# A two-layer hybrid block with a routed expert layer: gate products spread over 78 expert tiles, 30 gathers ahead, picks over 192 pairs

## The chip, the core and the metric

The kernel runs on one core of a Trainium2 chip. The metric is the device time of one execution in microseconds (us). The core has a matrix engine (TensorE, PE; its weight loads are shown as PEld), VectorE (DVE), ScalarE (ACT), GpSimd (POOL), SyncE (SP), which here only issues transfers, and 16 DMA engines. SBUF has 128 partitions; PSUM, into which the matrix engine writes, has 8 banks of 512 fp32 words in each partition.

## What is computed

Two layers over 512 tokens of width 1024. Each layer is a token mixer (a projection, a chunked scan, pooling, stick-breaking attention, an output projection) and then a routed expert layer, which the change is about. Cut to that:

```python
def peer_ffn(h, w_q, keys, u_tab, v_tab):
    q = (ht @ w_q).reshape(t, 8, 2, 128)
    sc = jnp.einsum('thid,hikd->thik', q, keys)           # 128 keys for each half
    top_s, top_i = lax.top_k(sc, 16)
    cand = top_s[:, :, 0, :, None] + top_s[:, :, 1, None, :]
    best_s, best_pos = lax.top_k(cand.reshape(t, 8, 256), 16)
    i1 = jnp.take_along_axis(top_i[:, :, 0], best_pos // 16, axis=-1)
    i2 = jnp.take_along_axis(top_i[:, :, 1], best_pos % 16, axis=-1)
    experts = i1 * 128 + i2                               # of 16384 experts
    gates = jax.nn.softmax(best_s, axis=-1)
    act = jnp.einsum('thkd,td->thk', u_tab[experts], h)
    return jnp.einsum('thk,thkd->td', gates * gelu(act), v_tab[experts])
```

## The kernel before

**Two ways to the experts.** For the first 160 tokens the rows of the chosen experts are fetched. Such a gather is an indirect DMA that brings one row of 1024 words (4 KB) for each partition, 512 KB in all. There are 160 of them from the u table and 160 from the v table in each layer (`UG`); DVE multiplies a u row by the token and sums it (`gather_u`), and adds a v row into a sum (`gather_v`). For the other 352 tokens (`TD`) all 16384 experts are computed. The u table comes as 128 tiles of 512 KB. In a **u tile** PE runs 24 matmuls of 352 columns: 8 steps of the inner dimension, each as high part by high part, high part by low part and low part by high part of the fp32 numbers. Behind the 128 u tiles come 128 v tiles of the same size.

**A u tile on each engine.** SP loads the tile into one of three raw slots (`load_w`). ACT copies it rounded to the high part (`hi`, line 765). DVE or, for tiles 2 to 38 of a layer, POOL subtracts to get the low part (`lo`, lines 1620 and 706). Both have two slots, so the parts of tile n+2 can be made only after tile n is done. PE multiplies (line 1047), and ACT takes the result through a gelu into `act_out` (line 977), from where SP stores two tiles at a time to DRAM.

**Routing.** In tiles 0 to 41 DVE turns the scores into experts and gates, in four groups of 128 tokens (`tt`). The step `picked` finds the index that belongs to each of the 128 chosen pairs of a token: a comparison (line 2212), a product (2214) and a sum (2218) over 128 x 16 elements, twice a group. Between them DVE consumes the first u gathers (`EARLY_GATHERS`: 14), of which POOL issues 16 in the tiles of `POOL_GATHER_AT`, each behind its low part. DVE then waits for POOL's last low part (tile 38) and takes over the low parts in its loop from tile 37 on, which in each turn n also consumes `U_GATHERS[n]` gathers.

**Gates.** A token's gates are needed as a matrix over all experts, 128 x 128 for each token. It is the product of two one-hot matrices, one of which carries the gates. Four tokens are a **quad**; there are 88. For a quad, DVE builds the one-hots (`one_hots`, line 2142, 1024 wide, one of `OH_SLOTS` = 4 slots), ACT scales one half by the gates (line 970, four instructions), PE runs four fp32 products of 128 x 128 (lines 1547 and 1561; the trace shows two instructions for each) behind the u tile, and ACT copies them from PSUM to `stages` (line 1001). `quads_of(n)` says which quads lie behind tile n: one or two by turns from tile 42 (`GATE0`) to 101. The gates of 224 of the 352 tokens go to DRAM in four chunks of 14 quads, each in four stores in four tiles one after another (`stores_of`), and come back in groups for the v tiles (`load_gates`, `load_acts`).

**Gather slots.** The gathered rows lie in a ring of five slots. POOL issues a gather once DVE has used the one five before (`s_gd`).

**PE's loops.** Tiles 42 to 97 are seven turns of a loop with eight tiles in it, then four tiles are written out, then a loop of two tiles runs to 127.

In every queue the instructions run in the order of the code: a wait on DVE for a gather holds all that DVE has behind it.

## Time and profile before

| | |
|---|---|
| median of three runs | 2907.31 us (2906.72 to 2907.58) |
| the profiled execution | 2909.28 us |
| its span, first to last instruction | 2907.5 us |
| busy: PE, PEld, DVE, ACT, POOL | 99%, 92%, 86%, 50%, 34% |
| granted PE clock, mean share of full | 0.997 |
| moved by DMA | 854.89 MB, mean 294 GB/s |

The stages, by the trace's time: layer 1 has its mixer to about 290 us, the key scores to 398, u tiles from 398 to 977 (the gate stretch from 569), v tiles to 1475. Layer 2 has the same at 1475 to 1719, 1809, 1809 to 2392 (gates from 1981) and 2890. In a row of a view, the engine, the line of the kernel, the operation and the tiles that it writes and reads come first; behind `<-` stands what ended a wait.

### The profile page before, as it was taken

The numbers are of one execution on the slowest core, as the hardware profiler recorded it, in microseconds if no ns is written. First come the engines' busy times: TensorE is split into PE (matmuls) and PEld (weight loads), VectorE is DVE, ScalarE is ACT, GpSimd is POOL, SyncE is SP. The second block draws the span as 40 slices with busy tenths as digits, with TensorE's granted clock in tenths as the row PEclk, the third lists the DMA queues.
The fourth block names the chain that finished last, engine by engine and source line by source line (L and its number), as shares of the span: only waits on it lengthen the run. The fifth ranks groups of instructions, "written<-read, shape, count | busy, mean of one in ns | idle before, by whom it ended". The sixth has DMA issues, their size and how long they took to land.

```text
span 2907.5 us, 49129 instructions
## 1 busy us (share of the span) xinstructions
PE 2864.6 (99%) x17864; PEld 2679.3 (92%) x17864; DVE 2495.4 (86%) x4770; ACT 1445.8 (50%) x2309; POOL 995.8 (34%) x773
## 2 busy tenths in 40 slices
PE   7999999999999999999999999999999999999998
PEld 4777789999999999999988788999999999999998
DVE  4667789799996899999986779989999879999998
ACT  3345234488883433334353532447888634333333
POOL 1000027644443343444400000675444433443442
PEclk9999999999999999999999999999999999999999
DMA  7435647899999999999932122679999999999996
GB/s 278 169 114 185 256 150 240 302 366 381 389 333 381 351 382 379 380 387 383 378 118 66 66 73 80 208 241 354 393 369 367 347 378 355 387 378 382 378 383 252
DMA packets 252524, 854.89 MB, mean 294 GB/s; under 512 B 25568, under 2 KB 58592, under 8 KB 245728
## 3 DMA queue, kind: packets, MB, share of 16 engines
q1 hardware_dynamic: 149280, 442.23, 41.7%
q0 software_dynamic: 98496, 381.73, 35.2%
q10 hardware_dynamic: 4608, 29.36, 2.4%
q8 instruction: 52, 0.85, 0.1%
q14 instruction: 88, 0.72, 0.1%
HBM read 777.06 MB, written 76.15 MB: 293 GB/s over the span
## 4 chain that ended last, share of the span: by engine, by line
PE 84%; DVE 7%; DMA 5%; ACT 2%; issue 1%; POOL 0%; SPq 0%; DVEq 0%; ACTq 0%; POOLq 0%
PE banks L1047 40%; PE banks L1579 30%; PE banks L1547 4%; DMA ring<-u,gidx 3%; DMA w_raw<-wst 2%; PE banks L1380 2%; DVE w_lo L1620 2%; PE banks L1117 2%; DVE ring L2120 1%; PE banks L1467 1%; PE banks L1063 1%; ACT w_hi L765 1%; DVE oneh L2142 1%; DMA ada_buf<-adaw 1%; DVE vacc L2132 0%
## 5 line engine op out<-in xcount | busy, mean ns | idle before, releaser
L765 ACT ACTIVATE w_hi<-w_raw 128x1024 fp32r<-128x1024 f32 x596 | 630.3, 1058 | 751.4 <-PE banks L1047 651.6
L1047 PE MATMUL banks<-hH,w_hi 128*128 128x352 f32 (+1 forms) x2528 | 867.4, 343 | 3.2 <-DVE w_lo L1620 1.9
L1620 DVE TENSOR_TENSOR w_lo<-w_raw,w_hi 128x1024 fp32r<-128x1024 f32 x522 | 639.0, 1224 | 263.6 <-ACT w_hi L765 259.9
L1047 PE MATMUL banks<-hH,w_lo 128*128 128x352 f32 (+1 forms) x2528 | 846.2, 335 | 0.0
L1047 PE MATMUL banks<-hL,w_hi 128*128 128x352 f32 (+1 forms) x2528 | 846.2, 335 | 0.0
L718 POOL DMA_INDIRECT ring<-v,gidx x320 | 396.8, 1240 | 593.3 <-DVE vacc L2132 532.3
L718 POOL DMA_INDIRECT ring<-u,gidx x320 | 395.4, 1235 | 466.3 <-DVE gact L2120 450.2
L1047 PEld LDWEIGHTS banks<-hH,w_hi 128*128 128x128 f32 x2528 | 475.5, 188 | 50.6 <-issue 20.6
L1579 PE MATMUL banks<-c_lo_late,w_hi 128*128 128x352 f32 x1536 | 494.2, 322 | 0.0
L1047 PEld LDWEIGHTS banks<-hH,w_lo 128*128 128x128 f32 x2528 | 474.8, 188 | 19.5
L1047 PEld LDWEIGHTS banks<-hL,w_hi 128*128 128x128 f32 x2528 | 475.8, 188 | 17.4 <-issue 0.5
L2132 DVE SCALAR_TENSOR_TENSOR vacc<-ring,gcoef,vacc 128x1024 f32<-128x1024 f32 x316 | 404.7, 1281 | 7.1
L2120 DVE CUSTOM_DVE_ANT_0 ring<-ring,banks 128x1024 f32<-128x1024 f32 x256 | 304.9, 1219 | 52.2 <-DMA ring<-u,gidx 27.8
L706 POOL TENSOR_TENSOR w_lo<-w_raw,w_hi 128x1024 fp32r<-128x1024 f32 x74 | 177.8, 2402 | 468.4 <-ACT w_hi L765 468.4
L1579 PE MATMUL banks<-c_hi_late,w_hi 128*128 128x352 f32 x1024 | 334.8, 327 | 2.6 <-DVE w_lo L1620 2.2
L1579 PE MATMUL banks<-c_hi_first,w_hi 128*128 128x352 f32 x1024 | 332.6, 325 | 0.0
L1579 PE MATMUL banks<-c_hi_first,w_lo 128*128 128x352 f32 x1024 | 331.0, 323 | 0.0
L1579 PE MATMUL banks<-c_hi_late,w_lo 128*128 128x352 f32 x1024 | 330.1, 322 | 0.0
L1579 PEld LDWEIGHTS banks<-c_lo_late,w_hi 128*128 128x128 f32 x1536 | 289.3, 188 | 0.0
L970 ACT ACTIVATE oneh<-oneh,idxT 128x128 f32<-128x128 f32 x704 | 214.9, 393 | 6.8 <-DVE oneh L2142 5.1
L2142 DVE TENSOR_TENSOR oneh<-iota,idxT 128x1024 f32<-128x1024 f32 x176 | 210.3, 1223 | 0.0
L1022 ACT ACTIVATE c_hi_late<-coef 128x352 fp32r<-128x352 f32 x128 | 63.8, 499 | 289.0 <-DVE coef L2292 289.0
(347 smaller groups left out, 4013.1 us busy)
## 6 DMA issues: line engine op xcount, KB each, us to landing
w_raw<-wst SPq DMA_DIRECT2D x596, 512.0 KB, 6.5
activations<-act_out SPq DMA_DIRECT2D x124, 352.0 KB, 8.2
act_in<-activations SPq DMA_DIRECT2D x62, 704.0 KB, 7.9
gate_matrices<-stages ACTq DMA_DIRECT2D x32, 896.0 KB, 9.3
gates<-gate_matrices SPq DMA_DIRECT2D x64, 448.0 KB, 9.6
ada_buf<-adaw POOLq DMA_DIRECT2D x24, 1024.0 KB, 6.8
nrm<-adaw POOLq DMA_DIRECT2D x8, 1024.0 KB, 5.2
pj<-adaw POOLq DMA_DIRECT2D x7, 1024.0 KB, 7.2
```

The costliest lines, as they stand in the source:

```text
L706: pool.tensor_tensor(w_lo[g % 2][:, :, :].rearrange("p a b -> p (a b)"), w_raw[:, g % RAWS, :], w_hi[g % 2][:, :, :].rearrange("p a b -> p ...
L718: pool.indirect_dma_start(out=ring[:, n % RING, :], out_offset=None, in_=rows[:, :], in_offset=bass.IndirectOffsetOnAxis(ap=gidx[:, k % UG ...
L765: nc.scalar.activation(w_hi[g % 2][:, :, :].rearrange("p a b -> p (a b)"), w_raw[:, g % RAWS, :], ACT.Copy).then_inc(s_wh, 1)
L970: ins = nc.scalar.activation(oh, oh, ACT.Copy, scale=idxT[:, 2, q * QUAD + t:q * QUAD + t + 1])
L1022: nc.scalar.activation(c_hi[(b + 2) % GROUP], coef[:, b % 2, :], ACT.Copy).then_inc(s_chi, 1)
L1047: last = mm(bank[s][:, 0:t.stop - t.start], a[s][:, k, :], b[:, k, t], start=(k == 0 and a is w_hi and b is hH), stop=(k == KT - 1 and a i ...
L1547: last = mm(bank[2 + u % 2][:, t * P:(t + 1) * P], oneh[u % OH_SLOTS][:, 0, t, :], oneh[u % OH_SLOTS][:, 1, t, :], start=True, stop=True)
L1579: last = mm(bank[k][:, TG:T], w[j % 2][:, k, :], c[j], start=(first and w is w_hi and c is c_hi), stop=(final and w is w_lo))
L1620: v.tensor_tensor(w_lo[g % 2][:, :, :].rearrange("p a b -> p (a b)"), w_raw[:, g % RAWS, :], w_hi[g % 2][:, :, :].rearrange("p a b -> p (a ...
L2120: v.tensor_tensor_reduce(ring[:, n % RING, :], ring[:, n % RING, :], rhs, 1.0, 0.0, ALU.mult, ALU.add, gact[:, k:k + 1]).then_inc(s_gd, 1)
L2132: ins = v.scalar_tensor_tensor(acc[:, :], ring[:, n % RING, :], gcoef[:, k:k + 1], acc[:, :], ALU.mult, ALU.add)
L2142: v.tensor_tensor(oneh[q % OH_SLOTS][:, :, :, :], iota[:, :].unsqueeze(1).unsqueeze(1).broadcast_to(full), idxT[:, 0:2, q * QUAD:(q + 1) * ...
```

## The change

Quads lie behind tiles 42 to 119, one a tile, and two in ten of them (`DOUBLE`). PE's loop holds 16 tiles and runs four times, and 14 tiles are written out. The one-hots have three slots, at another place. The first 30 u gathers of a layer land in 12 slots inside `stages`, which is unused until the first copies, and no longer in the ring; POOL issues 26 of them in tiles 11 to 38, DVE uses 20 in the routing stretch and the other ten in tiles 37 to 41. In DVE's loop the one-hots come ahead of the gathers. SP's first loads for the v tiles move from tiles 110, 112 and 116 to 116, 124 and 126. `picked` leaves out, for the eight best pairs, the indices that they can't have: 8 x 8 + 8 x 16 = 192 in place of 256 for each head, in two instructions in place of one. The matrices of a quad are laid out in PSUM by token in layer 1 (as before) and by expert in layer 2, where PE so writes with a step of four words; the copy to `stages` writes four neighbouring words at a time in both.

```diff
--- before.py
+++ after.py
@@ -94,9 +94,11 @@
 GATE0 = 42
-GATE1 = 102
-GATE_LOOP = 8
-OH_SLOTS = 4
+GATE1 = N_KEYS - 8
+GATE_LOOP = 16
+GATE_LOOPS = 4
+DOUBLE = [*range(7, 72, 8), 75]
+OH_SLOTS = 3
 
@@ -108,8 +110,8 @@
     i = n - GATE0
-    first = i // 2 * 3 + i % 2
-    return [q for q in ([first] if i % 2 == 0 else [first, first + 1]) if q < QUADS]
+    first = i + len([d for d in DOUBLE if d < i])
+    return [first, first + 1] if i in DOUBLE else [first]
 
@@ -138,19 +140,22 @@
 GATHERS = 2 * UG
-EARLY_GATHERS = (0, 4, 5, 5)
+EARLY_GATHERS = (0, 6, 7, 7)
 EARLY = sum(EARLY_GATHERS)
-POOL_GATHER_AT = [12, 13, 14, 15, 16, 20, 21, 22, 23, 28, 29, 30, 31, 32, 36, 37]
+AHEAD = 30
+AHEAD_SLOTS = 12
+AHEAD_FROM = 4
+AHEAD_SET = 4
+POOL_GATHER_AT = [11, 12, 13, 14, 15, 16, 17, 18, 19, 20, 21, 22, 23, 24, 25, 26, 27, 28, 29, 30, 31, 33, 34, 35, 37, 38]
 U_GATHERS = [0] * N_KEYS
 for _n in range(GATHER0, GATE0):
-    U_GATHERS[_n] = 1 if _n % 2 else 2
-for _n in range(GATE0, GATE1):
-    U_GATHERS[_n] = 2 if len(quads_of(_n + 1)) < 2 or _n % 4 == 2 else 1
-for _n in range(GATE1, N_KEYS - 1):
-    U_GATHERS[_n] = 2 if _n % 5 in (1, 3) else 1
-U_GATHERS[GATE1 + 4] = U_GATHERS[GATE1 + 14] = 1
-assert sum(U_GATHERS) + EARLY == UG and U_GATHERS[N_KEYS - 1] == 0, sum(U_GATHERS)
-POOL_GATE_LO = []
+    U_GATHERS[_n] = 2
+assert EARLY + sum(U_GATHERS) == AHEAD and len(POOL_GATHER_AT) <= AHEAD and POOL_GATHER_AT[-1] < GATHER0 + 2
+for _n in range(GATE0, N_KEYS - 1):
+    U_GATHERS[_n] = 1 if len(quads_of(_n + 1)) > 1 or _n == N_KEYS - 2 or _n % 2 and _n % 3 and _n + 1 < GATE1 else 2
+for _n in range(N_KEYS - 4, GATE0, -9):
+    U_GATHERS[_n] -= sum(U_GATHERS) > UG - EARLY and U_GATHERS[_n] > 1
+assert sum(U_GATHERS) + EARLY == UG and U_GATHERS[N_KEYS - 1] == 0, (UG - EARLY, sum(U_GATHERS))
 V_GATHERS = [0] + [2 if _b % 4 == 3 or _b in (33, 65, 97) else 1 for _b in range(1, N_KEYS - 1)] + [0]
@@ -397,11 +402,24 @@
         r3 = ExitStack()
-        oneh = [sb(f"oneh{s}", [P, 2, QUAD, P], where=r3) for s in range(2)]
+        sb("r3_gates", [P, GSTORED * GROUP * GCHUNK], where=r3)
+        oneh = [sb("oneh0", [P, 2, QUAD, P], where=r3)]
+        sb("r3_low", [P, 2048 - 1024 - GSTORED * GROUP * GCHUNK], where=r3)
         stages = sb("stages", [P, 2, N_KEYS, GWIDE], where=r3)
-        sb("r3_idx", [P, 20256 - 18432], where=r3)
-        oneh += [sb(f"oneh{s}", [P, 2, QUAD, P], where=r3) for s in range(2, OH_SLOTS)]
+        sb("r3_route", [P, 19776 - 18432], where=r3)
+        oneh += [sb(f"oneh{s}", [P, 2, QUAD, P], where=r3) for s in range(1, OH_SLOTS)]
         r3.close()
+
+        def gather_slot(l, k):
+
+            if k < AHEAD:
+                i = AHEAD_FROM + k % AHEAD_SLOTS
+                return stages[:, i // 8, :, :].rearrange("p e t -> p (e t)")[:, i % 8 * D:(i % 8 + 1) * D]
+            return ring[:, (l * (GATHERS - AHEAD) + k - AHEAD) % RING, :]
+
+        def by_expert(l, q):
+
+            return bank[2 + q % 2][:, :].rearrange("p (t e) -> p e t" if l == 0 else "p (e t) -> p e t", t=QUAD)
 
...
@@ -549,6 +567,7 @@
         s_g = [sem(f"gathered{s}") for s in range(RING)]
+        s_ga_in = [sem(f"gathered_ahead{s}") for s in range(AHEAD_SLOTS // AHEAD_SET)]
         s_gd = sem("gathered_used")
@@ -574,6 +593,16 @@
 
+        def gather_sem(l, k):
+
+            if k < AHEAD:
+                i = k % AHEAD_SLOTS // AHEAD_SET
+                uses = [j for j in range(AHEAD) if j % AHEAD_SLOTS // AHEAD_SET == i]
+                landed = len([j for j in uses if j // AHEAD_SLOTS <= k // AHEAD_SLOTS])
+                return s_ga_in[i], 16 * (l * len(uses) + landed)
+            n = l * (GATHERS - AHEAD) + k - AHEAD
+            return s_g[n % RING], 16 * (n // RING + 1)
+
         block = ctx.enter_context(nc.Block())
@@ -634,15 +663,15 @@
                         sp.dma_start(keys[:, :, :], keysT[l]).then_inc(s_keys, 16)
-                    if n == U0 + GATE1 + 8:
-
+                    if n == EV0 - 12:
                         for s in range(2):
                             sp.wait_ge(s_gst[s], (l + 1) * (GSTORED // 2) * STORES * 16)
+                        load_gates(l, 0)
+                    if n == EV0 - 4:
+
                         sp.wait_ge(s_gv, (l + 1) * QUADS + 2)
                         load_acts(l, 1)
-                    if n == U0 + GATE1 + 10:
-                        load_gates(l, 0)
-                    if n == U0 + GATE1 + 14:
+                    if n == EV0 - 2:
                         load_gates(l, 1)
@@ -709,16 +738,17 @@
 
-                n = l * GATHERS + k
-                if n >= RING:
-                    pool.wait_ge(s_gd, n - RING + 1)
+                if AHEAD_SLOTS <= k < AHEAD:
+                    pool.wait_ge(s_gd, l * GATHERS + k - AHEAD_SLOTS + 1)
+                if k >= AHEAD + RING:
+                    pool.wait_ge(s_gd, l * GATHERS + k - RING + 1)
                 if k == HK:
                 pool.indirect_dma_start(
-                    out=ring[:, n % RING, :], out_offset=None, in_=rows[:, :],
+                    out=gather_slot(l, k), out_offset=None, in_=rows[:, :],
                     in_offset=bass.IndirectOffsetOnAxis(ap=gidx[:, k % UG:k % UG + 1], axis=0)
-                ).then_inc(s_g[n % RING], 16)
+                ).then_inc(gather_sem(l, k)[0], 16)
 
@@ -735,19 +765,8 @@
                         gather(l, POOL_GATHER_AT.index(n - U0))
-                k = len(POOL_GATHER_AT)
-                used = EARLY
-                for n in range(GATHER0, GATE1):
-                    used += U_GATHERS[n]
-                    if n + 2 in POOL_GATE_LO:
-                        pool.wait_ge(s_wl, l * STREAM + U0 + n + 2)
-                        lo(l, U0 + n + 2)
-                    while k < used + RING:
-                        gather(l, k)
-                        k += 1
-                while k < GATHERS:
+                for k in range(len(POOL_GATHER_AT), GATHERS):
                     gather(l, k)
-                    k += 1
 
...
@@ -999,8 +1019,7 @@
                         nc.scalar.activation(
-                            home[:, :, i * QUAD:(i + 1) * QUAD].rearrange("p e t -> p t e"),
-                            bank[2 + q % 2][:, :].rearrange("p (t e) -> p t e", t=QUAD),
+                            home[:, :, i * QUAD:(i + 1) * QUAD], by_expert(l, q),
                             ACT.Copy).then_inc(s_gv, 1)
@@ -1534,7 +1553,14 @@
                 steps.settle()
-                per = GATE_LOOP // 2 * 3
+                per = GATE_LOOP // 8 * 9
+                def gate_quad(u):
+
+                    oh = oneh[u % OH_SLOTS]
+                    for t in range(QUAD):
+                        last = mm(by_expert(l, u)[:, :, t], oh[:, 0, t, :], oh[:, 1, t, :], start=True, stop=True)
+                    last.then_inc(s_gm, 1)
+
                 def gate_tiles(i, tiles):
@@ -1543,12 +1569,9 @@
                             pe.wait_ge(s_gv, l * QUADS + u + 1 + i * per)
-                            for t in range(QUAD):
-                                last = mm(bank[2 + u % 2][:, t * P:(t + 1) * P], oneh[u % OH_SLOTS][:, 0, t, :],
-                                          oneh[u % OH_SLOTS][:, 1, t, :], start=True, stop=True)
-                            last.then_inc(s_gm, 1)
-
-                loops = (GATE1 - GATE0) // GATE_LOOP
+                            gate_quad(u)
+
+                loops = GATE_LOOPS
                 with pe.Fori(0, loops) as i:
@@ -1557,10 +1580,7 @@
                         pe.wait_ge(s_gv, l * QUADS + u + 1)
-                        for t in range(QUAD):
-                            last = mm(bank[2 + u % 2][:, t * P:(t + 1) * P], oneh[u % OH_SLOTS][:, 0, t, :],
-                                      oneh[u % OH_SLOTS][:, 1, t, :], start=True, stop=True)
-                        last.then_inc(s_gm, 1)
+                        gate_quad(u)
                 with pe.Fori(GATE1 // 2, N_KEYS // 2) as i:
@@ -2114,22 +2134,22 @@
 
-                    n = l * GATHERS + k
-                    dve.wait_ge(s_g[n % RING], (n // RING + 1) * 16)
+                    dve.wait_ge(*gather_sem(l, k))
                     rhs = banks[:, 6:8, :].rearrange("p a t -> p (a t)") if k < HK else htok2[:, :]
-                    v.tensor_tensor_reduce(ring[:, n % RING, :], ring[:, n % RING, :], rhs, 1.0, 0.0,
-                                           ALU.mult, ALU.add, gact[:, k:k + 1]).then_inc(s_gd, 1)
+                    row = gather_slot(l, k)
+                    v.tensor_tensor_reduce(row, row, rhs, 1.0, 0.0, ALU.mult, ALU.add, gact[:, k:k + 1]).then_inc(s_gd, 1)
 
                     n = l * GATHERS + UG + k
-                    dve.wait_ge(s_g[n % RING], (n // RING + 1) * 16)
+                    dve.wait_ge(*gather_sem(l, UG + k))
+                    row = gather_slot(l, UG + k)
                     acc = vacc if k < HK else vacc2
                     if k in (0, HK):
-                        ins = v.tensor_scalar(acc[:, :], ring[:, n % RING, :], gcoef[:, k:k + 1], None, ALU.mult)
+                        ins = v.tensor_scalar(acc[:, :], row, gcoef[:, k:k + 1], None, ALU.mult)
                     else:
                         dve.wait_ge(s_gd, n)
-                        ins = v.scalar_tensor_tensor(acc[:, :], ring[:, n % RING, :], gcoef[:, k:k + 1], acc[:, :],
+                        ins = v.scalar_tensor_tensor(acc[:, :], row, gcoef[:, k:k + 1], acc[:, :],
                                                      ALU.mult, ALU.add)
@@ -2209,13 +2229,23 @@
                                         (col_at, iota[:, 0:TOPK], ALU.is_equal, row_at))[a]
-                    link(v.tensor_tensor(pk, at.unsqueeze(2).broadcast_to([P, HK, TOPK]),
-                                         of.unsqueeze(1).broadcast_to([P, HK, TOPK]), op))
-                    link(v.tensor_tensor(pk4, pk4, rows.unsqueeze(2).broadcast_to(full), ALU.mult))
+                    boxes = [(slice(0, 8), 8), (slice(8, TOPK), TOPK)]
+                    by_rank = lambda t: t.rearrange("p (h k) -> p h k", h=PH)
+                    for ranks, w in boxes:
+                        box = [P, PH, 8, w]
+                        ins = v.tensor_tensor(pk4[:, :, ranks, 0:w], by_rank(at)[:, :, ranks].unsqueeze(3).broadcast_to(box),
+                                              of[:, 0:w].unsqueeze(1).unsqueeze(1).broadcast_to(box), op)
+                    link(ins)
+                    for ranks, w in boxes:
+                        ins = v.tensor_tensor(pk4[:, :, ranks, 0:w], pk4[:, :, ranks, 0:w],
+                                              rows[:, :, 0:w].unsqueeze(2).broadcast_to([P, PH, 8, w]), ALU.mult)
+                    link(ins)
                     if a == 0 and tt >= 2:
                         dve.wait_ge(s_rtt, l * (NT - 1) + tt - 1)
-                    link(v.reduce_sum(route[:, a, :], pk, AX.X))
+                    for ranks, w in boxes:
+                        ins = v.reduce_sum(by_rank(route[:, a, :])[:, :, ranks], pk4[:, :, ranks, 0:w], AX.X)
+                    link(ins)
 
@@ -2304,21 +2334,18 @@
                 for n in range(GATHER0, N_KEYS):
-                    for _ in range(U_GATHERS[n]):
-                        gather_u(k)
-                        k += 1
                     if n == GATE0 - 1:
                         one_hots(q)
+                    for _ in range(U_GATHERS[n]):
+                        gather_u(k)
+                        k += 1
                     if n == N_KEYS - 2:
                         coefs(n - (N_KEYS - 2))
-                    if n + 2 not in POOL_GATE_LO:
-                        if n + 1 in POOL_GATE_LO:
-                            dve.wait_ge(s_wl, l * STREAM + U0 + n + 2)
-                        lo(l, U0 + n + 2)
+                    lo(l, U0 + n + 2)
                     if n >= N_KEYS - 2:
```

## Rows read from the trace of the kernel before

**Rows 1.** Busy time by stage: window, its length, each engine's busy time, PE clock, DMA.

```profile
398.00:570.00 172.00, 171.59 (x1066) 166.03 (x1063) 151.00 (x500) 73.84 (x102) 114.61 (x62) 1.00 0.72 233
570.00:875.00 305.00, 304.16 (x2120) 303.34 (x2119) 288.67 (x357) 267.41 (x558) 135.68 (x106) 1.00 0.97 368
875.00:978.00 103.00, 103.00 (x652) 103.00 (x652) 74.50 (x102) 39.10 (x57) 41.09 (x35) 1.00 1.00 381
...
1985.00:2290.00 305.00, 303.07 (x2104) 302.51 (x2103) 285.52 (x354) 265.17 (x553) 136.43 (x104) 0.99 0.97 363
```

**Rows 2.** Chain that ended last, merged: start us, length us, what.

```profile
561.79 11.73 PE banks L1047 x72
...
585.06 3.80 PE banks L1047 x24
...
590.64 3.81 PE banks L1047 x24
...
595.34 3.81 PE banks L1047 x24
...
875.09 102.61 PE banks L1047 x648
...
1981.31 4.25 PE banks L1047 x24
...
2289.63 102.61 PE banks L1047 x648
```

**Rows 3.** The same chain, where layer 2 loses time.

```profile
1968.47 10.21 DMA ring<-u,gidx
...
2135.74 17.93 DMA ring<-u,gidx
...
2154.92 2.29 DVE oneh L2142 x2
...
2160.39 4.92 PE banks L1047 x24
```

**Rows 4.** Busy time in shorter windows, columns as in rows 1.

```profile
600.00:620.00 20.00, 20.00 (x142) 20.00 (x140) 20.00 (x27) 17.68 (x39) 9.83 (x8) 1.00 0.93 341
...
720.00:740.00 20.00, 20.00 (x141) 20.00 (x140) 15.99 (x20) 17.49 (x37) 7.64 (x6) 1.00 1.02 420
...
900.00:930.00 30.00, 30.00 (x191) 30.00 (x190) 22.00 (x31) 11.29 (x16) 13.37 (x11) 1.00 1.03 406
```

**Rows 5.** Transfers of the page: issuer, count, KB each, median us to landing.

```profile
activations<-act_out SPq DMA_DIRECT2D x124, 352.0 KB, 8.2
...
gate_matrices<-stages ACTq DMA_DIRECT2D x32, 896.0 KB, 9.3
```

**Rows 6.** Timeline of ACT and POOL in layer 2's routing: start us, length us.

```profile
1850.23 1.06 ACT L765 ACTIVATE w_hi<-w_raw 128x1024 fp32r<-128x1024 f32 x1 [2.71 <-PE banks L1047]
...
1851.43 2.40 POOL L706 TENSOR_TENSOR w_lo<-w_raw,w_hi 128x1024 fp32r<-128x1024 f32 x1 [1.73 <-ACT w_hi L765]
...
1857.85 0.95 POOL L718 DMA_INDIRECT ring<-u,gidx  x1
```

**Rows 7.** Groups by line, DVE, 570 to 875 us: count, busy us, mean ns, idle.

```profile
L2142 DVE TENSOR_TENSOR oneh<-iota,idxT 128x1024 f32<-128x1024 f32 x88 | 105.1, 1223 | 0.0
```

**Rows 8.** Waits of DVE, 410 to 570 us: us in total, times, longest.

```profile
DVE ring L2120 <- POOL w_lo L706: 11.5, 1, 11.5
```

**Rows 9.** Groups by line, DVE's picks, 398 to 570 us.

```profile
L2214 DVE TENSOR_TENSOR pick<-pick,banks 128x2048 f32<-128x2048 f32 x8 | 18.3, 2288 | 0.3
```

**Rows 10.** Groups by line, ACT, 570 to 875 us.

```profile
L1001 ACT ACTIVATE stages<-banks 128x512 f32<-128x512 f32 x87 | 94.8, 1167 | 0.0
...
L977 ACT ACTIVATE act_out<-banks 128x352 f32<-128x352 f32 x59 | 26.3, 446 | 0.6 <-DMA activations<-act_out 0.6
```

**Rows 11.** Instructions of the gather line, 875 to 978 us: issue to landing.

```profile
DMA to landing us min/median/max: 5.5/7.7/9.1
```

**Rows 12.** All waits of DVE, 875 to 980 us.

```profile
DVE w_lo L1620 <- ACT w_hi L765: 31.1, 27, 2.1
```

5 lines of the change are left out of this document (3 added, 2 removed).

## Prediction

> **What bounds the kernel now.** I read the busy time by stage first [rows 1]. In both layers, from the start of the expert-score stage (398 and 1809 us) to the end of the second expert stage, TensorE (PE) works in nearly every microsecond: 304.2 of 305.0 in the gate stretch of layer 1, 303.1 of 305.0 in layer 2, all of the 103.0 behind it in layer 1. So the time there is that of the PE instructions, and what can be gained is only what PE loses between them. A PE busy time is blind to short losses, so the chain of waits is read next, for the pitch of the tiles [rows 2]. A u tile with nothing behind it takes 3.80 us (102.61 for 27). With one quad of one-hot products it takes 4.70 (590.64 to 595.34), with two 5.58 (585.06 to 590.64). One quad is thus 0.89 us wherever it lies. Sixty tiles from tile 42 on, of which 30 carry one quad, 29 two and one none, should take 30 x 4.70 + 29 x 5.58 = 302.8 up to the last of them. In layer 1 the chain has tile 40 at 561.79 and tile 101 at 875.09: 313.3, less two bare tiles (7.6) leaves 305.7, so **2.9 us are lost**. In layer 2 tile 42 stands at 1981.31 and tile 101 at 2289.63: 308.3, **5.5 us lost**. Some 0.3 of each is a change of datatype or rounding. The 26 tiles behind lose nothing.
>
> Where the loss comes from shows in the chain [rows 3]. A gather issued at 2135.7 takes 17.9 us to land, VectorE (DVE) stands before it, the two one-hot builds queued behind the gather (2.29 us) come late, and PE stands before these. In layer 2 the tile after that has 4.92 in place of 3.81. The DMA rate tells why [rows 4]: around 730 the 16 engines move 420 GB/s at a share of 1.02, around 610 only 341 at 0.93. The high stretches are those in which a gate chunk is stored, four stores of 896 KB each [rows 5].
>
> The routing stretch has another pace, seen in the timeline of layer 2 [rows 6]: ScalarE (ACT) makes the high part in 1.06 us, GpSimd (POOL) the low part in 2.40, and with both hand-overs 4.1 us go by before the tile after the next may start, against 3.8 of PE work. The gathers (0.95 us) lie in POOL's gap behind the low part.
>
> **The change, part by part.**
>
> *Quads over 78 tiles.* 68 tiles with one and 10 with two: 68 x 4.70 + 10 x 5.58 = 375.4, plus 8 bare tiles at 3.80 = 30.4, together 405.8. Before it was 302.8 + 27 x 3.80 = 405.4 for the same 86 tiles. PE's work is the same: **0**. What it alters is DVE. One of its 1024-wide instructions takes 1.22 us [rows 7], overlapping its neighbour, so that they follow each other at 1.14 (two one-hots in 2.29 [rows 3]). Four tiles of before hold 6 one-hots, 4 low parts and 7 gathers, 17 x 1.14 = 19.4 us of 20.6, 94%. After, a one-quad tile holds 1 + 1 + 1.6 on average, 4.1 of 4.70, 87%. The idle that was at tiles 102 to 127 is shared out.
>
> *One-hots ahead of the gathers on DVE.* The one-hots for tile n+1 are no longer queued behind gathers that may be late, so PE's wait for them [rows 3] should go. The low part is still behind them. The third slot instead of the fourth makes DVE wait for quad q-3, which PE finished two tiles before: nothing.
>
> *The chunk stores stay.* With 4.70 rather than 5.14 us a tile, the four stores of a chunk come closer. Bytes in such a tile: one weight tile and 1.6 gathers of 524 KB, 180 KB of activations, 918 KB of gates, together 2.46 MB in 4.70 us = 523 GB/s against 420. Before: 2.75 x 0.524 + 0.18 + 0.92 = 2.54 MB in 5.14 = 494. So the bursts are steeper, and weight tiles can be late in them too. DVE has 0.6 us of slack a tile to catch up, before 0.3. Bounds: all of 2.9 + 5.5 gone, or none of it. I take **-1.5 in layer 1 and -3.5 in layer 2**.
>
> *30 gathers ahead.* Ten more are issued in the routing stretch, one in nearly each tile, where the DMA share is 0.72 [rows 1]. Each is behind a low part on POOL, in a gap of 1.4 us or more for its 0.95 plus dispatch [rows 6]. From the 13th on each waits for the use of the gather twelve before; by tile 23 (about 489 us) DVE has used six, so POOL is not held. DVE now idles 11.5 us at tile 38 of layer 1 [rows 8], and finds ten landed rows when it starts again; ring gathers 30 to 34 wait for nothing. In layer 2 the chain at this place goes through a gather of 10.21 us [rows 3]. I take **-1**, bounds 0 and -2.
>
> *Picks over 192 pairs.* Six passes of 2048 elements at 2.29 us a tile group [rows 9] become twelve of 512 and 1024. Between 1.22 us for 1024 elements and 2.29 for 2048 lies 1.04 ns an element; 1536 elements in two passes, each overlapping its neighbour, cost about 1.8, so 0.5 x 6 x 4 = 12 us of DVE a layer. Six more gathers (6.8 us) use part of it. All of it falls into the idle before tile 38: **0** on the path.
>
> *Gate copies.* A copy takes ACT 1.17 us for 512 columns written in single scattered words, a plain pass of 352 takes 0.45 [rows 10], which would be 0.65 for 512. In runs of four it should come between: up to 0.5 us x 88 a layer of ACT, which is not on the path: **0**. In layer 2 the price is moved to PE: its products now go to PSUM with a step of four words. No row shows that. Below, 0: a column of these fp32 products takes 0.89 us / (8 x 128) = 0.87 ns, while a column of the 352-wide ones takes 3.80 / (24 x 352) = 0.45 ns, so there is room. Above, ACT's ratio of 1.8, taken as a doubling: 88 x 0.89 = 78 us. I take 0, as the nearest row is PE's own. A rule speaks against it. The Trainium skill, "SBUF — State Buffer", section "Door 1: The DMA port swizzle", says of PSUM that its lines hold two fp32 words and that "any non-contiguous PSUM access pattern significantly slows down matmuls". No row of this trace shows such a product; by that sentence layer 2 would be slower.
>
> *The tail.* Tiles 119 to 126 take 14 gathers where 11 were. At 3.80 us, a tile with two needs 3 x 0.524 + 0.18 = 1.75 MB, 461 GB/s against those 420, and SP's loads of activations (0.72 MB) and of a gate group (0.46), before at tiles 110 and 116, now fall there as well. Before, this stretch ran at up to 406 GB/s [rows 4], its gathers landed in 7.7 us [rows 11], and DVE waited for none of them, only for high parts [rows 12]. With five slots, two a tile leave 7.6 to 9 us to land. Shortage: 0.37 us a tile for 5 tiles plus 2.8 for the loads = 4.7 us, less what the full ring (2.6 MB, 6 us) covers. Bounds 0 and +4.7 a layer; I take **+1.5 a layer**, as the ring is in front but its last slots are needed at once. SP's waits (stores landed, last quad taken) are over when it reaches them, so the weight loads behind are not held.
>
> *PE's loop* is 16 tiles long and runs 4 times, in place of 8 tiles 7 times. At the returns of before the pitch is that of any tile: 0.
>
> **Sum.** -5 - 1 + 3 = -3. The profiled execution took 2909.3 (span 2907.5 and 1.8 around it), 2.0 above the median 2907.3. So 2906.3 for such an execution, **2904.3** as a median.
>
> **Rivals.** *A, the stalls vanish and the tail is free:* -2.9 - 5.5 - 2 = -10.4, less 0.6 of rounding: 2897.5. For it, DVE's slack is doubled and one-hots come first; against it, bursts are steeper. *B, the tail and the bursts starve DVE or the weight path:* the place is tiles 119 to 127, the price 4.7 a layer, nothing gained at the bursts: +9.4 - 1 = 2915.7. It decides once the ring's five rows are used up before tile 124. *C, strided PSUM writes slow PE in layer 2:* up to 2907.3 + 78 - 3 = 2982; a tenth of that already makes +5. It decides if a line step costs more than the 0.87 ns of a column. *D, it doesn't do what it says:* DVE's slack is filled by waits for high parts and the same bursts stall as before: 2907.3, within the forecast's bounds.
>
> **Chances.** Forecast and D, 2901.5 to 2913.1 (0.2% is 5.8 us, about what a measurement can tell here): 0.52. A 0.23. B 0.15. C 0.10. Faster 0.23, same 0.52, slower 0.25. The range 2897 to 2917 holds the forecast, A and B.
>
> **What would show it.** Right: a one-quad tile pitch of 4.70 all along in both layers; PE's waits for one-hots gone; DVE's waits for gathers moved from the chunk stores to tiles 119 to 127; the copies of line 1001 under 0.9 us. Wrong: quads of layer 2 above 0.9 us (C), PE gaps of over 1 us at tiles 119 to 127 (B), POOL waiting in tiles 23 to 38 so that low parts are late, or a pitch in the routing stretch other than 3.9 to 4.1.

## The result and the profile after

The changed kernel takes 2948.8 us (median of four runs, 2938.4 to 2952.3) against 2907.4 us before (four runs, 2906.7 to 2910.4). The ratio is 1.0137 with an interval of 1.0123 to 1.0150: **1.4% slower**, where 0.1% faster was forecast. The profiled execution after took 2938.4 us (span 2936.6), the one before 2909.3, so 29.1 us have to be found in the two traces. It is the fastest of the four; what the others lost beyond it, up to 13.9 us, no trace shows.

The busy time by stage, kernel after. Columns: window, its length, busy time and instructions of PE, PEld, DVE, ACT, POOL, then PE clock, DMA share, GB/s. The windows are: routing (tiles 0 to 41), gate stretch (42 to 118), tail (119 to 127), in layer 1 and then in layer 2.

```profile
397.30:572.00 174.70, 171.53 (x1063) 166.38 (x1060) 150.19 (x540) 73.63 (x101) 123.75 (x72) 1.00 0.76 262
572.00:957.20 385.20, 385.20 (x2547) 385.20 (x2545) 328.19 (x401) 252.64 (x589) 137.72 (x115) 1.00 0.94 339
957.20:999.60 42.40, 38.48 (x227) 38.22 (x226) 28.54 (x42) 14.83 (x25) 20.24 (x16) 0.96 0.99 372
1833.40:2008.60 175.20, 171.34 (x1046) 165.13 (x1046) 152.73 (x542) 74.10 (x102) 123.74 (x72) 1.00 0.76 261
2008.60:2379.40 370.80, 370.44 (x2545) 370.18 (x2545) 327.33 (x401) 252.90 (x589) 139.87 (x115) 1.00 0.96 352
2379.40:2421.40 42.00, 38.22 (x228) 37.80 (x227) 28.49 (x42) 14.91 (x25) 21.11 (x16) 0.92 1.01 392
```

Three things stand out against [rows 1]. The routing takes 174.7 and 175.2 us in place of 171.5 and 172.8, with 3.2 to 3.9 us in which PE does nothing. The nine tiles of the tail take 42.4 and 42.0 us; before they took nine bare pitches, 34.2 us, in both layers (now one quad of 0.9 us stands there too). And the gate stretch of layer 1 takes 385.2 us with PE busy in all of it, while that of layer 2, with the same work, takes 370.8. The third is the largest, and no engine's idle time shows it. By differences of tile starts: routing +3.3 and +2.4 us; tile 42 to the v tiles +19.6 in layer 1 and +2.0 in layer 2; between the stages 2.8 more and 1.0 less. The 2.8 us stay unexplained: from the v tiles of layer 1 to tile 0 of layer 2 this trace takes 833.8 us, the other 19 of this case 828.8 to 833.1.

**The hole at tile 41.** The chain of work that ended last, and DVE's and POOL's timelines of the same place:

```profile
561.03 3.82 PE banks L1066 x24
564.93 1.06 ACT w_hi L784
566.00 1.94 issue
567.94 8.23 PE banks L1066 x48
```

```profile
558.60 1.22 DVE L1640 TENSOR_TENSOR w_lo<-w_raw,w_hi 128x1024 fp32r<-128x1024 f32 x1
564.32 1.22 DVE L2140 CUSTOM_DVE_ANT_0 stages<-stages,banks 128x1024 f32<-128x1024 f32 x1 [4.51 <-DMA stages<-u,gidx]
```

```profile
554.17 0.94 POOL L748 DMA_INDIRECT stages<-u,gidx  x1 [0.30 <-DVE gact L2140]
555.42 1.79 POOL L748 DMA_INDIRECT stages<-u,gidx  x1 [0.30 <-DVE gact L2140]
```

Gathers 24 to 27 share one semaphore (`AHEAD_SET = 4`), and DVE's product of row 24 waits until all four have landed. POOL issues the last of them only after its last low part, at 555.42; DVE's wait ends 8.9 us later, at 564.32. DVE stands 4.51 us, the low part behind it is late, and the chain crosses from ScalarE to tile 41 at 567.94.

**The tail.** The chain again, layer 1, and all waits from 955 to 1000 us (engine and line, what it waited for: us in total, times, longest):

```profile
962.27 8.01 PE banks L1066 x48
...
971.52 1.24 DVE w_lo L1640
...
973.20 16.34 DMA activations<-act_out
...
989.57 0.47 ACT act_out L997
...
990.17 9.58 PE banks L1066 x48
```

```profile
ACT w_hi L784 <- DMA w_raw<-wst: 11.7, 3, 7.7
PEld banks L1066 <- issue: 4.2, 1, 4.2
PE banks L1066 <- ACT act_out L997: 3.9, 1, 3.9
```

A store of activations takes 16.3 us to land, where the median before was 8.2 [rows 5]; ScalarE waits up to 7.7 us for a weight tile. Tiles 125 and 126 last 8.1 and 5.4 us in layer 1, 7.9 and 6.5 in layer 2, in place of 3.8. The first of each pair holds PE's pause, some 4.1 us in layer 1 and 4.0 in layer 2. The second waits for nothing: behind the pause the granted clock (third column from the end) reads 0.50, the lower of PE's two levels, 1.2 GHz, in layer 1 and then in layer 2.

```profile
990.00:993.00 3.00, 2.83 (x10) 2.86 (x11) 2.15 (x4) 1.09 (x3) 1.68 (x1) 0.50 0.97 381
2411.00:2414.00 3.00, 2.94 (x10) 2.94 (x11) 2.18 (x5) 1.25 (x3) 1.68 (x1) 0.50 1.04 417
```

The matmuls there stand 293 ns apart. That is 1.4 of the 5.5 us lost in layer 1 and 2.7 of the 6.7 in layer 2.

**The pitch.** The same chain in the gate stretch, layer 1 and then layer 2:

```profile
577.06 4.00 PE banks L1066 x24
581.06 0.89 PE banks L1561 x8
581.95 4.00 PE banks L1066 x24
585.94 0.89 PE banks L1561 x8
```

```profile
2013.43 3.81 PE banks L1066 x24
2017.23 0.89 PE banks L1561 x8
2018.12 3.80 PE banks L1066 x24
2021.92 0.89 PE banks L1561 x8
```

The quads take 0.89 us in both. The 24 matmuls of a tile take 4.00 us in layer 1, a pitch of 166.7 ns, and 3.80 in layer 2 and before [rows 2], 158.4 ns. The granted clock is 1.00 (2.4 GHz) in both, and PE waits for nothing. I call the first the slow pitch. In layer 1 it lasts from tile 41 to 127, 87 tiles of 0.19 us: 16.8 us.

**What did come.** The stalls of the gate stretch [rows 3] are gone: layer 1 has none, layer 2 about 0.6 us, where 2.9 and 5.5 us were lost. DVE's waits for gathers there come to 0.6 us. The copies of the gates, groups by line of layer 1, cost half of [rows 10]:

```profile
L1021 ACT ACTIVATE stages<-banks 128x512 f32<-128x512 f32 x86 | 49.8, 592 | 0.0
```

Sum over both layers: 3.3 + 2.4 (routing) + 16.8 (slow pitch) + 5.5 + 6.7 (tail) - 2.9 - 4.9 (stalls) + 1.8 (between the stages) = 28.7 of the 29.1 us.

### The profile page after: what moved, and what is told of

Its sections match the earlier page's. It is cut to its first block, busy times and chain, and to the rows that moved or that the text cites. A ratio compares the mean times of both kernels' runs of the same rounds, so it can differ in the third digit from the quotient of the medians.

```text
span 2936.6 us, 49074 instructions
## 1 busy us (share of the span) xinstructions
PE 2880.7 (98%) x17864; PEld 2694.6 (92%) x17864; DVE 2480.8 (84%) x4818; ACT 1368.0 (47%) x2309; POOL 977.1 (33%) x773
## 4 chain that ended last, share of the span: by engine, by line
PE 84%; DMA 7%; DVE 5%; ACT 3%; issue 2%; SPq 0%; DVEq 0%; ACTq 0%
PE banks L1066 43%; PE banks L1599 26%; PE banks L1561 5%; DMA w_raw<-wst 4%; PE banks L1399 2%; DVE w_lo L1640 1%; ACT w_hi L784 1%; PE banks L1136 1%; DMA activations<-act_out 1%; PE banks L1486 1%; DMA pj<-adaw 1%; DVE vacc L2152 1%; PE banks L1082 1%; DVE h L1658 0%; PE banks L1240 0%
## 5 line engine op out<-in xcount | busy, mean ns | idle before, releaser
L748 POOL DMA_INDIRECT ring<-u,gidx x260 | 314.0, 1208 | 508.4 <-DVE gact L2140 497.1
L2140 DVE CUSTOM_DVE_ANT_0 ring<-ring,banks 128x1024 f32<-128x1024 f32 x196 | 233.2, 1213 | 2.6 <-DMA ring<-u,gidx 2.6
L990 ACT ACTIVATE oneh<-oneh,idxT 128x128 f32<-128x128 f32 x704 | 222.1, 398 | 3.2 <-ACT stages L1021 3.2
L1599 PEld LDWEIGHTS banks<-c_hi_late,w_hi 128*128 128x128 f32 x1024 | 192.2, 188 | 9.1 <-issue 8.3
## 6 DMA issues: line engine op xcount, KB each, us to landing
gates<-gate_matrices SPq DMA_DIRECT2D x64, 448.0 KB, 10.3
```

Of the source, the lines that this page charges most:

```text
L748: pool.indirect_dma_start(out=gather_slot(l, k), out_offset=None, in_=rows[:, :], in_offset=bass.IndirectOffsetOnAxis(ap=gidx[:, k % UG:k ...
L990: ins = nc.scalar.activation(oh, oh, ACT.Copy, scale=idxT[:, 2, at:at + 1])
L1599: last = mm(bank[k][:, TG:T], w[j % 2][:, k, :], c[j], start=(first and w is w_hi and c is c_hi), stop=(final and w is w_lo))
L2140: v.tensor_tensor_reduce(row, row, rhs, 1.0, 0.0, ALU.mult, ALU.add, gact[:, k:k + 1]).then_inc(s_gd, 1)
```

## The experiments

All 18 kernels compute the whole result. Ratios are against runs of the kernel before on the same chip.

**e1, the changed kernel again,** to see whether the slow layer is always the first.

> The changed kernel once more, unaltered. Its first trace has three losses: PE idle for 3.1 us at tile 40 of each layer, 5.5 and 6.7 us at the last u tiles, and, in layer 1 alone, a pitch of 166.7 ns between 352-column matmuls in place of 158.4 from tile 41 to 127 (+16.8 us). Theory: the two idle times belong to the order of the work and come back within 1 us. Open: if the slow pitch belongs to the code of layer 1, it is there again and layer 2 is free of it (span near 2937). If it is a state that PE falls into by chance at an idle time, it may be absent, or be in layer 2, and the span is 2920 to 2953.

2936.1 us, ratio 1.0095 (1.0075 to 1.0115). Layer 1 is fast, layer 2 is slow from tile 60 to 126. The hole (7.2 and 7.0 us for tile 40) and the long tiles 125 and 126 are in both layers, as in the first trace. So hole and tail belong to the program, while the layer and the tile at which the slow pitch begins change from execution to execution.

**e2, a semaphore for each gather slot; e3, a lighter tail as well.** e2 is one line; e3 adds these:

```diff
-AHEAD_SET = 4
+AHEAD_SET = 1
...
+for _n in range(GATE1 - 1, N_KEYS - 2):
+    U_GATHERS[_n] = 1
+for _n in (43, 59, 67, 83, 91, 107):
+    U_GATHERS[_n] += 1
```

> The changed kernel with one semaphore for each of the 12 slots of the early gathers (AHEAD_SET 1 in place of 4), so that VectorE waits for the row it uses and not for the last of a set of four. Theory: the idle time of 3.1 us at tile 40 is that wait, and goes to under 1 us in each layer: -5 us. If the slow pitch is started by that idle time, it goes too: -17 more, span near 2915. Rival: the wait is for the DMA rate behind nine issues in a row; then 2 us or more stay. Rival on the pitch: it has nothing to do with that idle time and stays in layer 1.

> As the one with own semaphores, and six of the u gathers of tiles 119 to 125 are used earlier, in tiles 43, 59, 67, 83, 91 and 107, so that a tail tile has one gather in place of two (SP's loads stay where they are). Theory: the 5.5 and 6.7 us at the last u tiles come from 461 GB/s asked against some 400 moved, with weight tiles landing in 14.7 us; with 324 GB/s asked they fall below 1.5 us each: another -10. With all three losses gone the time is near 2903; with the slow pitch left, near 2920. Rival: the loss is SP waiting for the last quad (3.9 us) with the store and the weight load queued behind; then 3 us or more stay in each layer.

e2: 2925.9 us (1.0060, 1.0040 to 1.0081). The hole is gone, tiles 0 to 41 take 171.1 and 171.5 us, and the chain runs through tile 40 and the next two:

```profile
560.88 0.33 PE banks L1508 x3
561.21 11.40 PE banks L1066 x72
```

The slow pitch doesn't go with the hole: layer 2 has it from tile 44 on.

e3: 2920.2 us (1.0042, 1.0025 to 1.0058). The tail is 37.0 us in both layers, and PE waits no more in it:

```profile
951.16 32.00 PE banks L1070 x192
983.16 3.86 PE banks L1603 x24
```

Eight tiles in 32.00 us are eight slow pitches; the ninth and the quad make up the rest. Two of the three parts are thus shown and mended. The third stays: layer 1 slow from tile 96, layer 2 from tile 40, to the v tiles each time, and nine runs from 2912 to 2931.

**e4, the kernel before with PE's loop of 16 tiles in place of eight** (`GATE_LOOP = 16`), since the changed kernel has that loop.

> The kernel before with PE's gate loop 16 tiles long, three turns and 12 tiles written out, in place of 8 long and seven turns; nothing else. Rule out or in: if the longer loop is what slows PE's pitch (instructions of 16 tiles fetched anew at each turn), tiles from 42 on show 166.7 ns and the time rises by up to 0.2 us a tile, 8 to 20 us. Theory: the loop costs nothing, 2907 within 3, pitch 158.4.

2909.9 us (1.0006, 0.9995 to 1.0016): the loop is not it. Up to here I held that a late tile starts the slow pitch, and that one and two quads by turns end it.

**e5 and e6, late tiles.** ScalarE's copy to the high part is made six times, so the tile comes 4.4 to 6.2 us late: in e5 tiles 60 and 110 of the kernel before, in e6 tile 60 of e3.

```diff
+                for _ in range(5 if n in (U0 + 60, U0 + 110) else 0):
+                    steps.link(nc.scalar.activation(w_hi[g % 2][:, :, :].rearrange("p a b -> p (a b)"), w_raw[:, g % RAWS, :], ACT.Copy))
```

> The kernel before, with ScalarE's rounding copy of the weights made six times in place of once for u tiles 60 and 110 of each layer, so that the matmuls of these two tiles start some 4 to 5 us late (nothing is left out of the result). Theory (a tile that starts late enters the slower matmul pitch, about 167 in place of 158 ns; the alternation of one and two quads ends it, bare tiles and tiles with one quad each keep it): after tile 60 at most three tiles are slow; after tile 110, where tiles are bare, all of the 17 up to the v tiles are slow in both layers, 17 x 0.19 us = 3.2 us a layer. Rival (the slower pitch comes by chance, or from the data movement of that stretch): no more slow tiles than in the kernel before at either place. The time rises by the four delays, about 4 x 4.5 = 18 us, to 2925 us, and by 6 us more (2931) under the theory.

> The kernel of e3 (own semaphores, light tail) with the same five extra copies for u tile 60 of each layer. Theory: the slower pitch begins at tile 60 or 61 in any layer in which it had not begun before, and stays up to the v tiles: about 67 slow tiles of the last 67 in both layers, and a time of about 2920 + 9 us of delays + 6 us = 2935. Rival (chance, or something that belongs to the tail): slow tiles begin at another tile than 60 to 62 in both layers, or end before the v tiles.

e5 (one run): 2939.2 us. Right behind tile 60 no tile is slow in either layer. Tile 110 itself begins at the lower clock after the pause (293 ns a matmul, a granted clock of 0.50 from 920 to 923 us); behind it all 17 tiles are slow in layer 1, none in layer 2. e6 (one run): 2925.7 us. Layer 2 is slow from tile 60 to 97, layer 1 not from 60 but from 98. So a late tile can start the slow pitch (two of six), it need not.

**e7, the spread of the quads undone**, all else of the change kept, with e2's semaphores:

```diff
-GATE1 = N_KEYS - 8
-GATE_LOOPS = 4
-DOUBLE = [*range(7, 72, 8), 75]
+GATE1 = 102
+GATE_LOOPS = 3
...
-    first = i + len([d for d in DOUBLE if d < i])
-    return [first, first + 1] if i in DOUBLE else [first]
+    first = i // 2 * 3 + i % 2
+    return [q for q in ([first] if i % 2 == 0 else [first, first + 1]) if q < QUADS]
```

> The changed kernel with the spread of the quads alone undone (one and two quads in turn in tiles 42 to 101 again, loops of eight tiles, SyncE's loads of the activations where they stood before), 30 gathers ahead and picks over 192 pairs kept, and a semaphore for each gather slot so that the idle time at tile 40 doesn't return. Theory (the spread is what costs: it fills the tail and lets the slower pitch persist): no slow pitch that lasts in tiles 42 to 101, 35 to 38 us from tile 119 to the v tiles, the stalls of the gate stretch smaller than before, and 2900 to 2907 us. Rival (the gathers ahead or the picks bring the slower pitch): 30 or more slow tiles between 42 and 101 in at least one layer, and 2915 us or more.

2903.1 us (0.9994, 0.9977 to 1.0010), in two groups: six runs from 2899.1 to 2903.5, four from 2913.3 to 2918.3. The profiled run is of the second group. Its layer 1 is slow from tile 40 to 127, with one and two quads by turns:

```profile
585.25 4.00 PE banks L1067 x24
589.24 1.78 PE banks L1562 x16
591.02 4.00 PE banks L1067 x24
```

My theory of the pattern fell here. The spread is not what makes the slow pitch last. Of 101 runs of the kernel before made beside these kernels, three took 2913 us or more, none over 2915.4.

**e8 to e11: is it how far PE's sequencer is ahead?** In the traces most starts stood at tiles whose work was released less than 0.3 us before its turn. Counted over all 20 traces, by the end of the tile's low part or of the scaled one-hots just ahead of it, these are 26 of 34 starts from tile 42 on, against 84 of 2479 tiles at which none began. And the kernel before releases its quads later than the changed one. In e8 and e10 (e3 and e7) the sequencer is held behind each tile until its 18th matmul is done, in e9 until the 6th; e11 is e7 with DVE's old order.

```diff
+                    if k == part:
+                        last.then_inc(s_part, 1)
...
+                def held_tile(n, s):
+                    project(l, U0 + n, s, tokens=slice(TG, T), part=5)
+                    pe.wait_ge(s_part, l * (N_KEYS - GATE0) + n + (1 - GATE0))
```

> The kernel of e3 with one wait more for each u tile from tile 42 on: TensorE's sequencer, which runs ahead of the matmuls, waits behind each tile until the 18th of its 24 matmuls is done before it goes on to the quads or the next tile. Theory (over the traces so far the slower pitch starts only in tiles whose work was released less than 0.3 us before its turn, 19 of 19 starts, and it ends in the gate stretch only where it was released less than 1.2 us before; released earlier than that, the state is kept): the release now comes some 0.6 to 0.8 us ahead of the quads or of the next tile, so no slow stretch lasts longer than about ten tiles; the tiles themselves become no longer; 34 to 35 us from tile 119 to the v tiles in place of 37; 2920 becomes about 2905 to 2910. Rival (the state has nothing to do with how far the sequencer is ahead): slow stretches of 30 tiles or more as in e3, and 2915 to 2925 us.

> The same instructions as in e8, but the wait is for the 6th matmul of the tile in place of the 18th, so that the sequencer is hardly held (2.5 us ahead of the tile's end). Theory: as e3, in at least one layer of the profile or in some of the timed runs slow stretches of 30 tiles or more, 2912 to 2930 us. If e8's gain came from the added instructions and not from how late the release is, this kernel is as fast as e8.

> The kernel of e7 with the wait of e8. In e7 six of ten runs took 2899 to 2904 us and four 2913 to 2918; the profiled one of these had one layer of 88 slow tiles. Theory: no lasting slow stretch, and so all runs at 2898 to 2905 us, about 5 us faster than before. Rival: some of the runs at 2913 us or more as in e7.

> The kernel of e7 with one thing put back as it was before the change: in each of the tiles 41 to 101 VectorE does the products of the gathered rows ahead of the one-hots of the next tile's quads, not behind them, so that the quads are released later. Theory: the quads are released some 0.6 to 1 us before their turn, as before the change, so no slow stretch lasts in tiles 42 to 101 and no run takes 2913 us or more; in return the short stalls of the gate stretch come back in part: 2902 to 2908 us. Rival (the lasting slow stretch comes from the gathers ahead or the picks): some runs at 2913 us or more.

| kernel | median us | runs | slow tiles in a row (profiled run) |
|---|---|---|---|
| e8 | 2919.7 | 2909 to 2930 | layer 2: 86 to 121 |
| e9 | 2917.7 | 2907 to 2923 | layer 2: 60 to 127 |
| e10 | 2901.8 | three at 2901 to 2902, two at 2913 and 2916 | layer 2: 40 to 103 |
| e11 | 2917.5 | four at 2898 to 2907, six at 2917 to 2937 | none |

The theory fell too: with the sequencer held the slow pitch lasts as long, and with the old order on DVE some runs are as slow as any. Its second half, that the slow pitch ends only where the release was less than 1.2 us ahead, didn't hold even in the trace of the kernel before: it ends in tile 76 of layer 2, whose quad was ready 2.1 us ahead. What is left between e11 and the kernel before are the one-hot buffers, the PSUM layout, the gathers ahead and the picks.

**e12 to e14: one part alone in the kernel before.** e12 takes the one-hot buffers:

```diff
-OH_SLOTS = 4
+OH_SLOTS = 3
...
-        oneh = [sb(f"oneh{s}", [P, 2, QUAD, P], where=r3) for s in range(2)]
+        sb("r3_gates", [P, GSTORED * GROUP * GCHUNK], where=r3)
+        oneh = [sb("oneh0", [P, 2, QUAD, P], where=r3)]
+        sb("r3_low", [P, 2048 - 1024 - GSTORED * GROUP * GCHUNK], where=r3)
         stages = sb("stages", [P, 2, N_KEYS, GWIDE], where=r3)
-        sb("r3_idx", [P, 20256 - 18432], where=r3)
-        oneh += [sb(f"oneh{s}", [P, 2, QUAD, P], where=r3) for s in range(2, OH_SLOTS)]
+        sb("r3_route", [P, 19776 - 18432], where=r3)
+        oneh += [sb(f"oneh{s}", [P, 2, QUAD, P], where=r3) for s in range(1, OH_SLOTS)]
```

> The kernel before with the one-hot buffers of the change alone: three in place of four, at the change's addresses, and the loop of 16 tiles that three buffers need (e4 has shown the loop alone to cost nothing). If the buffers are what lets the slower pitch last: some runs at 2915 us or more, and where the profiled run is one of them, 40 or more slow tiles in a row. If not: all runs between 2900 and 2915 us, as before. Fewer buffers alone can make the short stalls of the gate stretch longer: up to 5 us.

> The kernel before with the PSUM layout of the change alone: ScalarE copies a quad's gates to contiguous places, from a strided bank in layer 1, and in layer 2 TensorE's products write the bank strided (ScalarE's copy 0.59 in place of 1.17 us in both layers). If that lets the slower pitch last: some runs at 2915 us or more. If not: 2900 to 2915 us, and the median within 3 us of before, since ScalarE has time to spare in the gate stretch.

> The kernel before with the gathers of the change alone: 30 of them ahead in 12 slots in the stages, each with its own semaphore, and on VectorE the one-hots ahead of the gathered rows' products; four one-hot buffers, loops of eight tiles, the PSUM layout and the picks as before. If the gathers ahead and the earlier release of the quads let the slower pitch last: some runs at 2913 us or more and others at 2899 to 2904. If not: all at 2899 to 2906 us, since the stalls of tiles 43, 61 and 75 go, and this kernel is then the fastest of all.

e12: **2923.8 us, 1.0064 (1.0051 to 1.0078)**, six of seven runs at 2915.5 to 2934.1. e13: 2904.3 us, **0.9989 (0.9980 to 0.9997)**, twelve runs, none above 2912.4. e14: 2907.5 us, 0.9995 (0.9986 to 1.0004), eleven runs, none above 2912.7. The buffers alone bring the times above 2915 us; the PSUM layout and the gathers ahead don't. The gain forecast for e14 didn't come: tile 61 loses 0.2 us in both layers as before, tile 75 of layer 2 still 0.7. The picks were not taken alone; e18 below has them, and no run of it is above 2906.7 us. e12's profiled run was its fastest, but layer 2 shows five slow tiles, 71 to 75, that go on through quads and end at a stall of PE in tile 75 (the 0.04 of issue between its two quads, the second of which takes 1.13 in place of 0.89):

```profile
2130.96 4.00 PE banks L1049 x24
...
2136.74 4.00 PE banks L1049 x24
...
2152.29 3.99 PE banks L1049 x24
2156.28 0.90 PE banks L1549 x8
2157.18 0.04 issue
2157.22 1.13 PE banks L1549 x8
2158.35 3.80 PE banks L1049 x24
```

**e15 to e18: their number or their places?** e15 has three buffers at the first three of the four old places. e16 has four; its whole diff is

```diff
-        sb("r3_idx", [P, 20256 - 18432], where=r3)
+        sb("r3_idx", [P, 19776 - 18432], where=r3)
```

e17 is e3 (quads spread) with the four buffers of before, e18 is e7 (quads not spread) with them.

> The kernel before with three one-hot buffers at the first three of its four addresses, loops of 16 tiles. If the number of buffers matters: as e12, most runs at 2915 us or more. If their addresses matter: all runs at 2901 to 2915 us.

> The kernel before with four one-hot buffers, the third and fourth of them at the addresses of the change's second and third (480 words a partition lower). If the addresses matter: some runs at 2915 us or more. If the number matters: all runs at 2901 to 2915 us.

> The kernel of e3 (one quad a tile, own semaphores, light tail) with four one-hot buffers at the addresses of before, loops of 32 tiles, and the stored gates loaded at tile 124 in place of 116, since the first buffer lies where they go. If three buffers are the cause: no slow stretch of more than ten tiles between tiles 42 and 119, and a median of 2903 to 2910 us in place of 2920 (some us of stalls stay in the tail). If the steady one-quad pattern lets the slower pitch last by itself: 30 slow tiles or more in a layer, 2915 us or more.

> The kernel of e7 with the four one-hot buffers and the loops of eight tiles of before: of the change it keeps 30 gathers ahead (a semaphore for each slot), the one-hots ahead of the products, the PSUM layout and the picks. If three buffers are the cause: all ten runs or so between 2898 and 2905 us (e7's six faster runs), 0.2 to 0.3% faster than before. If not: two groups of runs again, one at 2913 us or more.

| kernel | median us | runs | ratio, interval |
|---|---|---|---|
| e15 | 2915.6 | 10: 2907 to 2926 | 1.0025, 1.0011 to 1.0039 |
| e16 | 2925.0 | 4: 2918 to 2934 | 1.0068, 1.0048 to 1.0087 |
| e17 | 2920.8 | 4: 2920.0 to 2921.6 | 1.0044, 1.0029 to 1.0060 |
| e18 | 2902.4 | 11: 2900.8 to 2906.7 | 0.9984, 0.9975 to 0.9993 |

**e16 settles the cause**: the kernel before, with its third and fourth one-hot buffers 480 words (1920 bytes) lower in each partition and nothing else changed, loses 17.6 us. My either-or was wrong, though: e15 is slow as well. One rule fits both. It is read from all traces tile by tile: which buffer does the first quad behind a slow tile read? Where PE had no stall in the tile,

- the third or fourth buffer at its old place: the slow pitch ended with that tile in 14 of 14 cases (tiles 44, 62, 71, 76 and others, six traces);
- any other buffer or place: it went on in 695 cases and ended in three, and in those three the second quad was ready only some 0.16 us before its turn.

Only the first quad counts. In 25 cases the second one behind the tile read the third or fourth buffer at its old place (21 of them in e15), and the slow pitch went on. Behind a bare tile no buffer is read, and there it can last too (e14, tiles 113 to 127 of layer 1).

In e15 and e12 the first quad of a tile is always quad 0 or 1 of three, never the third buffer, so nothing ends the slow pitch; in the changed kernel all three buffers lie elsewhere. Two chains, layer 2 of the kernel before (tiles 42 to 45) and layer 1 of e16 (from the end of tile 75):

```profile
1986.44 4.00 PE banks L1047 x24
1990.44 1.78 PE banks L1547 x16
1992.22 3.99 PE banks L1047 x24
1996.21 0.89 PE banks L1547 x8
1997.11 3.81 PE banks L1047 x24
```

```profile
736.23 4.00 PE banks L1047 x24
740.22 0.89 PE banks L1547 x8
741.11 4.00 PE banks L1047 x24
745.11 2.00 PE banks L1547 x16
747.11 3.80 PE banks L1047 x24
```

In the first the quad at 1996.21 is quad 3, the first to read the fourth buffer: the next tile takes 3.81. (Quad 2, the second of the two at 1990.44, had read the third.) In e16 the slow pitch began at tile 62 (672.2) and went on through 19 quads, all four buffers among them. It ends at 747.11, behind two quads that took 2.00 in place of 1.78: a stall of 0.22 us ended it, not a buffer.

e17 bears the rule out with the quads spread: no slow stretch is longer than five tiles, three of its five ends stand behind a quad in the third buffer, and the other two at stalls. Its time is lost elsewhere. Four buffers need a loop of 32 tiles, and at that loop's only return PE waits 4.8 us; timeline of PE, layer 1:

```profile
721.08 1.95 PE L1563 MATMUL banks<-oneh 128*128 128x128 f32 x16
727.84 0.63 PE L1068 MATMUL banks<-hH,w_hi 128*128 128x352 f32 x1 [4.82 <-issue]
```

Tiles 73 and 74 last 10.7 and 6.6 us (9.9 and 7.3 in layer 2) in place of 5.6 and 4.7, together 13.9 us. In tile 74 PE waits for nothing, but the granted clock reads 0.50 behind the pause (727.8 to 731 us). Without the 13.9 us e17 would be at about 2907, an estimate.

**e18 beats both kernels**, the one before by 0.16% (0.07 to 0.25): all eleven runs lie between 2900.8 and 2906.7 us. It is the change without the spread, with the four buffers at their old places and a semaphore for each gather slot.

## Why the prediction was wrong, step by step

- *What bounds it* held: PE is busy nearly all the time, and the sum over pitches and quads is the time. The step that failed is the one behind it, that 24 matmuls take 3.80 us wherever they run. [Rows 2] had the other value in it: 4.25 us for tile 42 of layer 2 at 1981.31, of which I took all over 3.80 for a stall. It holds 0.2 us of slow pitch, and tiles 43 and 44 behind it have 4.00. In all, three tiles in layer 1 and five in layer 2 of the gate stretch before were slow, 0.6 and 1.0 of the 2.9 and 5.5 us. The 4.92 of [rows 3] isn't all waiting either: its first seven matmuls stand 290 ns apart, at a granted clock of 0.50 (2160.3 to 2162.3 us), 1.0 us more.
- *One-hots ahead of the gathers* came as forecast: "PE's wait for them should go". I took -1.5 and -3.5; it was -2.9 and -4.9, the slow tiles before among them.
- *Three slots in place of four*: "makes DVE wait for quad q-3, which PE finished two tiles before: nothing". True of DVE, and the costliest line of the prediction. The new buffers let a slow pitch last that the old places ended; +16.8 us in the profiled run, 14.9 and 17.6 in the medians of e12 and e16. That an address could have a price was in no rival.
- *30 gathers ahead*: "finds ten landed rows when it starts again". By then POOL has issued only 26, so at most six unused rows, the last of them issued at 552.92, as DVE starts again. I counted gathers against DVE's use and neither against POOL's list nor with the shared semaphore: +5.7 us in place of -1. e2 shows it. Mended, the routing takes 171.1 and 171.5 us, 0.4 and 1.3 less than before: so -1.7 came, within the bounds of the -1.
- *Picks* cost nothing on the path, as forecast: in e2 DVE still waits 11.7 us before tile 38, as in [rows 8], with six more gathers behind it. *Gate copies* were worth more than the 0: e13, with them alone, is 0.11% faster, and its tiles 43, 61 and 75 have no stall in either layer. That the quads there had waited for ScalarE's copies is the likely reason; no run shows it.
- *Rival C* fell: layer 2's products, with a step of four words in PSUM, take 0.89 us a quad at 2017.23, as in layer 1. The Trainium skill, "SBUF — State Buffer", section "Door 1: The DMA port swizzle", says that "any non-contiguous PSUM access pattern significantly slows down matmuls"; for these fp32 products the trace doesn't show it.
- *The tail*: rival B's mechanism came, at 5.5 and 6.7 us a layer where I took 1.5 and bounded it by 4.7. PE's pause itself, 4.1 and 4.0 us, was inside the bound. The term missing from the sum is what PE does behind it: 1.4 and 2.7 us more at the lower clock. I had looked for the shortage at the gathers; the chain ends it at a store of `act_out` that lands after 16.3 and 15.6 us. e3, with fewer gathers there, takes 37.0 us without a pause.
- *PE's loop* of 16 tiles: 0 was right. The traces of the changed kernel show nothing at its returns, those of e4 and e12 0.2 to 0.6 us at the first. At 32 tiles it would have been 7 us a layer (e17).

What stays open: why that place in SBUF ends the slow pitch, and what it is inside PE. No run tells. Nor do they say why it starts at some late tiles and not at others.

## What to carry to other kernels

Write the same instructions' times from two places side by side before you take one as fixed: an engine that is 100% busy at a granted clock of 1.00 can still run 5% slower for 87 tiles. Where runs of one kernel fall into groups 15 us apart, compare distributions, and treat buffer addresses as a part of the change: put them back alone, and move them alone. And when work is issued ahead, count what has been issued and what its semaphore waits for, not what fits in the slots.
